# Norms of a two-layer transformer step on one core: row sums by transposes instead of ones-columns and diagonals

## The reference, cut to what matters

```
def rms_norm(x, g):
    y = x * rsqrt(mean(x * x, axis=-1) + 1e-6)
    return y * g

x = x + 0.5 * rms_norm(swiglu(rms_norm(x, g[0]), w1, w3, w2), g[1])   # FFN
x = x + rms_norm(mixer(rms_norm(x, g[2])), g[3])                      # attention
```

## Time and profile before

| | |
|---|---|
| three runs | 1874.56 us median, 1873.05 to 1874.79 |
| profiled execution, first to last instruction | 1870.9 us |
| PE busy | 1857.0 us, 99% |
| PEld busy | 1704.5 us, 91% |
| DVE busy | 1361.3 us, 73% |
| ACT busy | 868.4 us, 46% |
| POOL busy | 49.6 us, 3% |
| DMA | 93 GB/s, queue 1 at 32.7% of the 16 engines |

### The profile page before, as it was taken

How to read it: one execution, slowest core, us unless ns; L and a number is a source line. 1 busy time by engine, 2 the same in 40 slices (tenths; PEclk the granted TensorE clock), 3 DMA queues, 4 the chain that set the end, 5 groups by cost and what they waited for, 6 DMA issues and landing times.

```text
span 1870.9 us, 31002 instructions
## 1 busy us (share of the span) xinstructions
PE 1857.0 (99%) x12243; PEld 1704.5 (91%) x12243; DVE 1361.3 (73%) x1885; ACT 868.4 (46%) x1258; POOL 49.6 (3%) x55
## 2 busy tenths in 40 slices
PE   8999999999999999999999999999999999999999
PEld 7899988988889899998898999989988898999888
DVE  6899962487656889992278999922888488999623
ACT  6444452355545544452255444522666464444422
POOL 0000000011100000000000000000000000000000
PEclk9999999999999999999999999999999999999999
DMA  6243343222213333333313343433222232343431
GB/s 179 81 113 107 95 118 100 83 84 71 77 57 102 91 91 93 109 97 111 107 52 112 91 112 91 114 98 103 63 63 57 68 89 78 105 112 96 118 101 46
DMA packets 339463, 174.64 MB, mean 93 GB/s; under 512 B 11070, under 2 KB 337836, under 8 KB 339372
## 3 DMA queue, kind: packets, MB, share of 16 engines
q1 hardware_dynamic: 338656, 172.25, 32.7%
q10 hardware_dynamic: 716, 1.11, 0.2%
HBM read 171.24 MB, written 2.10 MB: 93 GB/s over the span
## 4 chain that ended last, share of the span: by engine, by line
PE 89%; DVE 8%; ACT 2%; issue 1%; DMA 0%; POOL 0%; SPq 0%; DVEq 0%; ACTq 0%
PE acc L1877 21%; PE acc L1879 21%; PE acc L1878 21%; PE duo L1877 8%; PE duo L1878 8%; PE duo L1879 8%; DVE sqs L1284 1%; PE duo L1905 1%; DVE xg L1208 1%; DVE y L1231 1%; DVE xT L1238 1%; DVE wl L1164 1%; PE acc L2137 1%; DVE mx L1530 1%; PE duo L1912 0%
## 5 line engine op out<-in xcount | busy, mean ns | idle before, releaser
L1877 PE MATMUL acc<-xg,wh 128*128 128x256 f32 (+1 forms) x1552 | 488.1, 314 | 1.3 <-DVE xg L1208 1.0
L1879 PE MATMUL acc<-xg,wl 128*128 128x256 f32 (+1 forms) x1552 | 481.7, 310 | 0.0
L1878 PE MATMUL acc<-xg,wh 128*128 128x256 f32 (+1 forms) x1552 | 481.6, 310 | 0.0
L1164 DVE TENSOR_TENSOR wl<-raw,wh 128x1024 fp32r<-128x1024 f32 (+2 forms) x198 | 228.9, 1168 | 117.9 <-ACT wh L645 117.6
L1877 PEld LDWEIGHTS acc<-xg,wh 128*128 128x128 f32 x1552 | 296.0, 191 | 20.4 <-issue 2.2
L1878 PEld LDWEIGHTS acc<-xg,wh 128*128 128x128 f32 x1552 | 296.1, 191 | 16.6 <-issue 1.4
L1879 PEld LDWEIGHTS acc<-xg,wl 128*128 128x128 f32 x1552 | 296.0, 191 | 15.8
L1877 PE MATMUL acc<-hT,wh 128*128 128x512 f32 (+1 forms) x704 | 255.5, 363 | 0.0
L1878 PE MATMUL acc<-hT,wh 128*128 128x512 f32 (+1 forms) x704 | 255.3, 363 | 0.0
L1879 PE MATMUL acc<-hT,wl 128*128 128x512 f32 (+1 forms) x704 | 255.3, 363 | 0.0
L645 ACT ACTIVATE wh<-raw 128x1024 fp32r<-128x1024 f32 (+2 forms) x198 | 194.3, 1011 | 117.1 <-PE acc L1879 71.1
(11 more groups left out here) (287 smaller groups left out, 3229.8 us busy)
## 6 DMA issues: line engine op xcount, KB each, us to landing
raw<-in_ffn_w_dram SPq DMA_DIRECT2D x238, 512.0 KB, 4.1
raw<-in_ffn_w_dram SPq DMA_DIRECT2D x32, 384.0 KB, 3.4
raw<-in_moba_w_qkv_dram SPq DMA_DIRECT2D x24, 512.0 KB, 3.8
raw<-in_moba_w_o_dram SPq DMA_DIRECT2D x8, 512.0 KB, 3.8
raw<-in_mla_w_o_dram SPq DMA_DIRECT2D x8, 512.0 KB, 3.8
xin<-in_x_dram SPq DMA_DIRECT2D x4, 512.0 KB, 5.6
raw<-in_mla_w_dq_dram SPq DMA_DIRECT2D x4, 512.0 KB, 3.9
raw<-in_mla_w_uq_dram SPq DMA_DIRECT2D x8, 256.0 KB, 2.9
```

What stands on the lines that cost most here:

```text
L1164: v.tensor_tensor(wl[:, slot, 0:tiles], raw[:, slot, 0:tiles], f32(wh[:, slot, 0:tiles]), ALU.subtract).then_inc(w_lo, 1)
L1877: t.matmul(dst, w_h, m_h, start=start, stop=False)
L1878: t.matmul(dst, w_h, m_l, start=False, stop=False)
L1879: return t.matmul(dst, w_l, m_h, start=False, stop=stop)
```

## The change

- `mean` no longer multiplies with a column. It transposes each 128x128 block of squares through the identity, four transposes in a call, side by side in `norm_bank`. The tokens come to stand on the partitions and the features along the free axis.
- `norm_var` becomes a DVE `tensor_reduce` (add) over 512 elements a partition, in four groups of 128 or two of 256. It writes `var`. So do `xvar` and the last norm's half.
- `spread` transposes the column of `rtok`, read 128 times through a stride of zero, once for each block of 128 tokens: four transposes, or two for a half.
- `norm_diag`, `ones`, `mean_w`, `ckv_diag` and the semaphore `diag_ready` are gone.
- The 1/n is a scale of ACT's squares, the 1e-6 is added (as 1e-6/128) in an add of the partial sums that DVE makes anyway, which becomes a `scalar_tensor_tensor`. The factor 0.5 is multiplied once, near the start, into the gains of the FFN's post norms (one DVE instruction on 128x32 elements), and ACT waits for it before the first FFN.
- `query_var` is now two DVE instructions, a row sum and a `scalar_tensor_tensor`, with a semaphore between them. The two inner norms both use the scale for 256 features, and the factor 2 is corrected in `query_var` and `query_scale`.

```diff
             def add_square(n, i):
...
+                if i == 1 and n != N_CQ:
+
+                    ins = v.scalar_tensor_tensor(out=sumsq[:], in0=sumsq[:], scalar=EPS / P, in1=square_buf(n, i)[:],
+                                                 op0=ALU.add, op1=ALU.add)
...
             def norm_var(n, e=0, cols=slice(0, TS)):
 
                 dve.wait_ge(var_psum, EV0[n] + e + 1)
-                v.tensor_scalar(var[:, cols], norm_bank[e][:, cols], EPS, None, ALU.add).then_inc(var_ready, 1)
-
-            def norm_diag(n, e, factor, diag, cols=slice(0, TS)):
-
-                dve.wait_ge(rtok_ready, RT0[n] + e + 1)
-                w = cols.stop - cols.start
-                v.scalar_tensor_tensor(out=diag[:, cols.start * P:cols.stop * P].rearrange("p (t q) -> p t q", q=P),
-                                       in0=ident[:].unsqueeze(1).broadcast_to([P, w, P]), scalar=factor,
-                                       in1=rtok[:, cols].unsqueeze(2).broadcast_to([P, w, P]),
-                                       op0=ALU.mult, op1=ALU.mult).then_inc(diag_ready, 1)
+                row_sums(var[:, cols], e).then_inc(var_ready, 1)
+
+            def row_sums(dst, e):
+
+                return v.tensor_reduce(dst, norm_bank[e].rearrange("p (c k) -> p c k", c=dst.shape[1]), AX_X, ALU.add)
...
                 add_tail(n, 0)
                 post_var(n, 0)
-                post_diag(n, 0, factor)
                 split(u)
...
             dve.wait_ge(var_psum, EV0[N_PRE4] + 1)
-            v.tensor_scalar(xvar[:], aux[:, 0:TS], EPS, None, ALU.add).then_inc(r_ready, 1)
+            row_sums(xvar[:], 0).then_inc(r_ready, 1)
...
             def query_var():
                 dve.wait_ge(var_psum, EV0[N_CQ] + 1)
                 dve.wait_ge(r_ready, EV0[N_PRE4] + 1)
-                v.scalar_tensor_tensor(out=var[:], in0=xvar[:], scalar=EPS, in1=norm_bank[0][:, 0:TS],
+                step(row_sums(var[:], 0))
+                v.scalar_tensor_tensor(out=var[:], in0=xvar[:], scalar=EPS * QR / KVR, in1=var[:],
                                        op0=ALU.mult, op1=ALU.add).then_inc(var_ready, 1)
...
                 for c in cols:
-                    for i, src in enumerate(parts):
-                        ins = t.matmul(norm_bank[e][:, c:c + 1], src[:, c * P:(c + 1) * P], mean_w[width][:],
-                                       start=i == 0, stop=i == len(parts) - 1)
+                    for src in parts:
+                        ins = t.transpose(norm_bank[e][:, o:o + P], src[:, c * P:(c + 1) * P], ident[:])
+                        o += P
                 ins.then_inc(var_psum, 1)
 
-            def spread(n, e=0, cols=slice(0, S), diag=T[3]):
-
-                pe.wait_ge(diag_ready, SPREAD0[n] + e + 1)
-                t.matmul(norm_bank[e][:, cols], ones[:], diag[:, cols], start=True, stop=True).then_inc(r_psum, 1)
+            def spread(n, e=0, cols=range(TS)):
+
+                pe.wait_ge(rtok_ready, RT0[n] + e + 1)
+                for c in cols:
+                    ins = t.transpose(norm_bank[e][:, c * P:(c + 1) * P], rtok[:, c:c + 1].broadcast_to([P, P]),
+                                      ident[:])
+                ins.then_inc(r_psum, 1)
```

More of the change, by code:

```diff
@@ L128, in half @@
         return slice(e * HALF, (e + 1) * HALF)
+    SQ_SCALE = [D ** -0.5] * 14
+    SQ_SCALE[N_CKV] = SQ_SCALE[N_CQ] = KVR ** -0.5
+    assert D == 32 * 32 and KVR == 16 * 16 and QR == 2 * KVR
     X_LOAD, X_F0, X_MOBA, X_F1, X_F2, X_MLA, X_F3 = range(7)
@@ L663, in square @@
                     act.wait_ge(sumsq_added, A0[n] + i - bufs)
-                s.activation((square_buf(n, i) if i else sumsq)[:], src, SQUARE).then_inc(sq_ready, 1)
+                s.activation((square_buf(n, i) if i else sumsq)[:], src, SQUARE, scale=SQ_SCALE[n]).then_inc(sq_ready, 1)
             def y_tile(m, bank, g_post, cols=slice(0, S)):
@@ L677, in tail_square @@
                     act.wait_ge(unit_done, u_end - step * (LAST[n] - 1 - i))
-                s.activation(last_square(n, i)[:, half(e)], tail_banks(n, e)[i][:, half(e)], SQUARE
-                             ).then_inc(sq_last, 1)
+                s.activation(last_square(n, i)[:, half(e)], tail_banks(n, e)[i][:, half(e)], SQUARE,
+                             scale=SQ_SCALE[n]).then_inc(sq_last, 1)
             def tail_y(n, e, i, g_post):
@@ L696, in x_squares @@
                 for k in range(0, KD, KD // 2):
-                    s.activation(sqs[:, k:k + KD // 2, half(e)], xT[:, k:k + KD // 2, half(e)], SQUARE
-                                 ).then_inc(sq_ready, 1)
+                    s.activation(sqs[:, k:k + KD // 2, half(e)], xT[:, k:k + KD // 2, half(e)], SQUARE,
+                                 scale=SQ_SCALE[n]).then_inc(sq_ready, 1)
             def x_update(t, n, g_post, u, gcol, n_pre):
@@ L1283, in x_squares @@
                             dve.wait_ge(sumsq_added, A0[n] + 3 * e + step)
-                        v.tensor_tensor(sqs[:, 0:w, half(e)], sqs[:, 0:w, half(e)], sqs[:, w:2 * w, half(e)],
-                                        ALU.add).then_inc(sumsq_added, 1)
+                        if w > 1:
+                            ins = v.tensor_tensor(sqs[:, 0:w, half(e)], sqs[:, 0:w, half(e)], sqs[:, w:2 * w, half(e)],
+                                                  ALU.add)
+                        else:
+                            ins = v.scalar_tensor_tensor(out=sqs[:, 0, half(e)], in0=sqs[:, 0, half(e)], scalar=EPS / P,
+                                                         in1=sqs[:, 1, half(e)], op0=ALU.add, op1=ALU.add)
+                        ins.then_inc(sumsq_added, 1)
             def pre_norm(n, u):
@@ L1330, in ffn @@
                 if kv is not None:
-                    before, between, after = kv
+                    before, after = kv
                     before()
@@ L1350, in ffn @@
                 split(u + 9)
-                if kv is not None:
-                    between()
                 dve.wait_ge(xn_ready, 2 * nth + 2)
@@ L1892, in from_x, with mean @@
                 return lambda k: (buf[:, 0, k, cols], buf[:, 1, k, cols])
-            def mean(n, e=0, width=D, cols=range(TS), parts=None):
+            def mean(n, e=0, cols=range(TS), parts=None):
                 pe.wait_ge(sumsq_added, A0[n + 1] - (LAST[n] - 1 if LAST[n] and e == 0 else 0))
@@ L2002, in ffn @@
                     if st == KV_ST and i == 6:
-                        mean(N_CKV, width=KVR)
+                        mean(N_CKV)
                     if st == KV_ST and i == 8:
-                        spread(N_CKV, diag=ckv_diag)
+                        spread(N_CKV)
                     unit(u + i, acc[i % 4][:], from_x(xg))
@@ L2312, in _ @@
                 if h == 0:
-                    mean(N_CQ, width=QR)
+                    mean(N_CQ)
                 if h:
```

48 lines of the change are left out of this document (20 added, 28 removed).

## The result

The changed kernel takes 1863.53 us (median of 4 runs, 1862.69 to 1864.59), the kernel before 1873.81 us (4 runs on the same chip, 1873.05 to 1874.79): a ratio on record of 0.9947, 95% interval 0.9935 to 0.9959 (the quotient of the two medians is 0.9945). So it is shorter by half a percent, with the interval clear of 1. Run again later beside other kernels it took 1862.89 us (5 runs) against 1874.49 (9 runs), 0.9944 [0.993, 0.9957]. The forecast was 1864.3 us, in the direction named and within the range.

A forecast was written before the change was run, and what follows sets the result against it. TensorE's stream was taken to bound the kernel: 14.0 us gross, less 1.05, 0.1, 0.96, 1.18 and 0.46, leaves 10.25, so 1874.6 - 10.3 = 1864.3 us. Range 1860.5 to 1869; the forecast's own 1862.5 to 1866.5, chance 0.68.

The forecast's parts named there:

- The 3.7 us that I put around the span: Start and end of the execution: the runs' median lies 3.7 us above the profiled span, untouched by the change.
- Prices on TensorE: Mean 0.90 to 0.44 us, half spread 0.43 to 0.22, full spread 0.86 to 0.44; together 14.0 us saved gross.
- The rival of transposes that do not overlap: All 126 transposes in means and spreads hold TensorE's stream for 273 ns each: slower, 1882.4 us; chance 0.04.
- that of the dear column: Rival: the spreads' 46 stride-zero column transposes cost like matmuls, 5.3 us more, so 1869.6 us; chance 0.08.
- The row sum: On DVE, a row sum replaces each norm's small add, taking 0.68 us, +0.52 over the add.
- First half's saving swallowed by the second half's mean: In 5 residual updates the first-half spread's 0.21 turns into TensorE's wait for DVE at the second mean: -1.05 us.
- Second half's spread to the pre norm's mean: DVE's chain and TensorE's next matmul both start at the spread's end, so both move together and 0.3 of waiting stays.
- Pre norm's spread "covered": Between pre norm's mean and spread, 24 matmuls (2.9 us) hide row sum and POOL's power, even at twice its 0.70.
- Ahead of MLA: The xvar row sum delays a weights' low part; TensorE loses the mean's 0.46 and waits about 0.5: -0.96 us.
- First head of MLA: Row sum and second instruction delay kh; TensorE goes on 0.72 later instead of 0.46 earlier: -1.18 us.
- Last norm: Second half: the later row sum delays the final multiplications and store, so the mean's saving counts as 0: -0.46 us.
- The signs that I had named for being wrong: A spread waiting over 0.2 us for rtok, the residual's first product over 0.1 late, or transpose groups over 0.6 us.

The follow-up runs named there:

- the doubled groups: Three kernels, each the changed kernel with one kind of spread's transposes issued twice: first halves 1862.49 us, second halves 1863.04, pre norms and keys 1864.48.
- the doubled first halves: The changed kernel with the two transposes of the post norms' first-half spreads issued twice: 1862.49 us, one run; stream +0.32.
- the kernel with the spreads alone: The changed kernel, but with the means made as before, by one-column matmuls and a small add: 1869.82 us, ratio 0.9979 to before.
- The edit of the order: The changed kernel with MLA's xvar row sum behind the next weights' low part, and the first head's qh and kh moved earlier on DVE: 1862.14 us, ratio 0.9936.
- the means alone: The changed kernel, but with the factor spread as before, by DVE diagonals and a matmul with ones: 1868.34 us, ratio 0.9974 to before.

## Why the prediction was right, and where its steps were not

- *The bound.* "The time is the length of TensorE's stream": the stream became 10.4 (and 10.2 in the second execution) shorter, and the runs 10.3. The 3.7 us that I put around the span were wrong, though: the executions of the changed kernel lie 2.5 us above their own spans (1864.30 for 1861.8), and the rest of the 3.7 was a long start that the profiled execution of before did not have and the median of its three runs had (last section). It cancels in the difference of the two medians of four runs. The 1874.6 that I started from was a run with the long start, and that is the 0.8 us between the forecast 1864.3 and the measured 1863.53. Among the waits I also called the 1.4 us for `sqs` the one that belongs to the norms; the same view has 1.7 us in 5 places for `sumsq`, which the forecast counts only further down.
- *Prices on TensorE.* Four transposes 0.44, two 0.22, the stride-zero column like any other: measured wherever no wait stands beside them, and shown by the doubled groups. The rival of transposes that do not overlap is out with that, and so is that of the dear column.
- *The row sum*, 0.68: 0.69.
- *First half's saving swallowed by the second half's mean* (5 x 0.21): shown by the doubled first halves. The wait grew by 0.18 and not 0.21 in each, so 0.15 more arrived than forecast.
- *Second half's spread to the pre norm's mean*: this step failed. I wrote that "both move together and the 0.3 of waiting stays", with DVE free 0.1 us before the spread ends. I had followed DVE to its `y` only. Ahead of `y` it makes two low parts, and TensorE needs the second of them right behind the spread; with the row sum in front it ends 0.32 too late for the shorter spread. So each second spread costs 0.38 more than forecast (0.60 for 0.22), 1.9 in all. TensorE's stop there lets DVE catch up, and the wait ahead of the pre norm's mean is gone, 0.34 in each of five, 1.7. That the one follows from the other is borne out by the kernel with the spreads alone, where there is no stop and the wait stays at 1.24. So the two errors are one thing seen at two places, and nearly cancel.
- *Pre norm's spread "covered"*: nearly. I had allowed POOL twice the 0.70 of two columns; it took 1.91, since DVE no longer stood still beside it. Five times 0.11 to 0.13, about 0.6 us. That DVE's freedom has a price on POOL had no place in the forecast, although the keys' power in the trace of before (1.93) showed it.
- *Ahead of MLA*, -0.96: the place and the wait were right, the size a little high. TensorE's matmuls were 8.61 ahead of before behind the last pre norm's mean and 7.70 at the first product with the late `wl`, so 0.91 was lost there; 0.17 came back ahead of the inner mean, where the lead was 7.87, so 0.74 was lost for good. The edit of the order brought 0.60 of it back.
- *Behind the keys' norm*, nothing in the forecast: 0.37 was lost, at the wait for `xg` at 1030.78, and 0.39 in the second execution. With the spreads alone nothing is lost there, with the means alone 0.53. What makes that `xg` late I have not followed.
- *First head of MLA*, -1.18: the wrong wait, and mis-sized. I had looked at `kh` alone, but the row sum stands ahead of `qh` too, which had 0.36 us to spare before (it ended at 1363.07, and the product came at 1363.43); TensorE now waits 0.78 there, and the lead falls from 8.31 to 7.26. At `kh`, where I forecast a wait longer by 1.2, PEld's wait got shorter (0.5 before, 0.3 now) and 0.24 came back. DVE had 0.27 us of idle time ahead of `kh`, waiting for ACT, and the row sum filled it first: `kh` ends 4.21 us behind the inner mean's start where it was 3.85, 0.36 later and not 0.73. TensorE's next product began 0.35 later against that mean, which with the mean's own 0.46 makes 0.81; by the next post norm 0.47 of it was left. The other 0.34 came back in the later heads, between 1438.70 and 1446.66 (lead over before 7.50, then 7.87); by what, I have not followed.
- *Last norm*: the 0.1 for a first spread that waits for `rtok` did not come (0.22 measured). The last mean saved 0.45, of which I took nothing for the end; from the last mean to the end there are 7.43 us instead of 7.64, so 0.21 more arrived than forecast.

In the stream the errors are +1.7 (pre norms' means), +0.2 and +0.7 (MLA), +0.15 and +0.1 on one side and -1.9 (second spreads), -0.6 (POOL) and -0.37 (keys) on the other. They sum to nothing, and the forecast of 10.25 was right to 0.2 because they cancel. That is in good part luck: only the +1.7 and the -1.9 belong together.

The signs that I had named for being wrong did not catch this. No spread waited more than 0.2 us for `rtok`, `y` began right behind the second half's spread, and no group of transposes took more than 0.6 us without a wait in front of it. The signs of being right held for the transposes and the row sums, but not for `wl` ahead of MLA (0.73 and not nearly 1) and for `kh`.

## What to carry to other kernels

Where a stream is level with a second engine, list for each group that gets shorter *every* operand of the next two or three matmuls behind it, the weights' parts too, and not only the chain that the group itself belongs to. An instruction that is inserted eats the idle time ahead of the next one first (at `kh` here), so look for that idle time before you price it, and look at each operand behind the insertion and not at the last alone: ahead of `qh` DVE had no idle time. And an engine that stops waiting for another will run beside it: ask whether the two slow each other, as POOL's power was here. When a wait is left over at the end, look for idle time on the engine that it waits for: DVE's 1.5 us behind the row sum gave another 1.6 to 1.8 us, by order alone.

## What the runs showed of the hardware

POOL's power over 128x4 elements takes 1.01 or 1.02 us with DVE idle and 1.91 to 1.93 beside DVE's subtraction of two SBUF operands, in all five pre norms and in the keys' norm, whether one or two such subtractions follow each other. Over 128x2 elements it takes 0.70 with DVE idle and 0.87 beside DVE's `xg`, which reads SBUF alone; the 0.77 above is the mean of both. In both cases the power grows by nearly what is left of the one DVE instruction that runs when it starts: 0.90 for 1.04 left, 0.17 for 0.32 left.

In the first profiled execution of the changed kernel the first nineteen matmuls of 256 columns advanced by 0.21 us instead of 0.12 (the first of all by 0.35 instead of 0.19); timeline of TensorE, then the same place in the second execution of the same kernel:

```profile
11.51 0.41 PE L1875 MATMUL acc<-xg,wl 128*128 128x256 f32 x1
11.72 0.41 PE L1873 MATMUL acc<-xg,wh 128*128 128x256 f32 x1
11.94 0.41 PE L1874 MATMUL acc<-xg,wh 128*128 128x256 f32 x1
```

```profile
11.28 0.28 PE L1875 MATMUL acc<-xg,wl 128*128 128x256 f32 x1
11.40 0.28 PE L1873 MATMUL acc<-xg,wh 128*128 128x256 f32 x1
11.52 0.28 PE L1874 MATMUL acc<-xg,wh 128*128 128x256 f32 x1
```

The granted clock is given as 1.00 for this stretch in both (windows: stretch, PE busy and records, PEld, DVE, ACT, POOL, clock, DMA; first, then second execution):

```profile
10.90:15.10 4.20, 4.16 (x19) 4.19 (x20) 3.91 (x10) 4.13 (x9) 0.00 (x0) 1.00 1.15 302
```

```profile
10.90:15.10 4.20, 4.13 (x33) 4.04 (x34) 3.91 (x10) 4.16 (x9) 0.00 (x0) 1.00 1.16 307
```

By the pace, 0.21 and 0.12 are about what 256 columns take at 1.2 and at 2.4 GHz, so it looks like the lower of the clock's two levels, although the column does not say so; that is argued and not shown. It put the first mean 1.6 us later (33.30 against 31.68). Of the thirteen executions with a trace this is the only one with that start. The runs of one kernel fall into two groups about as far apart: 1864.30, 1862.76, 1864.59 and 1862.69 us for the changed one (spans 1861.8, 1860.3, 1862.1 and 1860.2), 1874.56, 1873.05, 1874.79 and 1873.06 for the one before. The profiled execution of the changed kernel is one of the long ones; that of the kernel before, with its first mean at 31.75, began like the short ones. That is why the spans differ by 9.1 us here, and by 10.5 with the second execution's 1860.4. The Trainium skill, "TensorE: Matmul & The Clock Gate", section Part 1: The HAM clock gate (the "warmup" mystery), says that the number of matmuls at the low clock at a kernel's start varies from run to run, which fits. That this start is also what parts the runs into two groups is argued from the spans, since only single executions have a trace. So for differences of a few us a span, or a median of three runs, is not a measure unless the start is looked at.
